# A block with two transformer layers, one core: the first feed-forward layer's down projection partly by seven products

## The reference, cut to what matters

```python
SEQ = 512
D_MODEL = 1024
D_FF = ((8 * D_MODEL // 3 + 255) // 256) * 256      # 2816
...
def first_block(x, positions, ...):
        ...
        x = x + rms_norm(y, post_mix_norm[l])
        h = rms_norm(x, pre_ffn_norm[l])
        f = (jax.nn.silu(h @ w_gate[l]) * (h @ w_up[l])) @ w_down[l]
        x = x + rms_norm(f, post_ffn_norm[l])
    return x
```

## Time and profile before

| | |
|---|---|
| median of 3 runs | 1816.99 us (1814.9 to 1817.48) |
| the profiled execution | 1819.24 us, of which its span is 1817.44 |
| TensorE, matmuls | busy 98% of the span, granted clock 0.998 of full |
| VectorE, ScalarE, GpSimd | busy 61%, 46%, 19% |
| transfers | 230.85 MB, mean 127 GB/s |

### The profile page before, as it was taken

One profiled execution on the slowest core, in us unless ns is written; L12 is line 12 of the kernel. 1 busy time (PEld: TensorE's weight loads), 2 busy tenths in 40 slices (PEclk: granted clock), 3 DMA queues, 4 the chain that ended last, 5 costly groups with the idle time before them and its releaser, 6 DMA issues.

```text
span 1817.4 us, 24673 instructions
## 1 busy us (share of the span) xinstructions
PE 1783.8 (98%) x9586; PEld 1452.3 (80%) x9586; DVE 1113.3 (61%) x1763; ACT 834.6 (46%) x1593; POOL 336.7 (19%) x404
## 2 busy tenths in 40 slices
PE   7999999999999999999999999999999999999998
PEld 7767898888888877878878786667788998888886
DVE  6655643233345787887778745677556357574747
ACT  5346533222224555554555544554435445342435
POOL 1503000000000046254462640000020012112120
PEclk9999999999999999999999999999999999999999
DMA  7211333323332454352443444233543248849482
GB/s 246 80 59 62 97 114 116 93 93 93 93 93 75 151 142 131 120 152 95 154 140 117 143 158 152 82 102 119 139 149 123 76 145 191 229 107 257 114 208 70
DMA packets 140419, 230.85 MB, mean 127 GB/s; under 512 B 27264, under 2 KB 59456, under 8 KB 139664
## 3 DMA queue, kind: packets, MB, share of 16 engines
q1 hardware_dynamic: 118944, 166.70, 29.2%
q0 software_dynamic: 20496, 60.10, 12.5%
q10 hardware_dynamic: 864, 2.49, 0.3%
HBM read 216.54 MB, written 12.71 MB: 126 GB/s over the span
## 4 chain that ended last, share of the span: by engine, by line
PE 78%; DVE 12%; DMA 3%; ACT 3%; issue 2%; POOL 1%; SPq 0%; DVEq 0%; ACTq 0%; POOLq 0%
PE m L2134 13%; PE m L2136 13%; PE m L2135 13%; PE m L2145 6%; PE m L2147 6%; PE m L2146 6%; PE s L2297 3%; DVE lo L1395 3%; DMA raw<-in_w_up_dram 3%; PE m L2269 2%; PE m L2242 2%; PE m L2244 2%; PE m L2243 2%; PE m L2271 1%; PE m L2270 1%
## 5 line engine op out<-in xcount | busy, mean ns | idle before, releaser
L2134 PE MATMUL m<-hH,hi 128*128 128x512 f32 (+1 forms) x1392 | 530.6, 381 | 3.2 <-DVE hL L1425 1.6
L2136 PE MATMUL m<-hH,lo 128*128 128x512 f32 (+1 forms) x1392 | 509.8, 366 | 0.0
L2135 PE MATMUL m<-hL,hi 128*128 128x512 f32 (+1 forms) x1392 | 509.1, 366 | 0.0
L1395 DVE TENSOR_TENSOR lo<-raw,hi 128x1024 fp32r<-128x1024 f32 x267 | 335.9, 1269 | 193.0 <-ACT hi L915 192.6
L915 ACT ACTIVATE hi<-raw 128x1024 fp32r<-128x1024 f32 x267 | 276.1, 1050 | 205.3 <-DMA raw<-in_w_up_dram 64.9
L2134 PEld LDWEIGHTS m<-hH,hi 128*128 128x128 f32 x1392 | 263.3, 189 | 51.2 <-issue 4.5
L2136 PEld LDWEIGHTS m<-hH,lo 128*128 128x128 f32 x1392 | 263.1, 189 | 43.4
L2135 PEld LDWEIGHTS m<-hL,hi 128*128 128x128 f32 x1392 | 263.7, 189 | 38.9
L2145 PE MATMUL m<-hi,hH 128*128 128x512 f32 (+1 forms) x320 | 133.8, 418 | 1.6 <-DVE lo L1395 1.6
L2147 PE MATMUL m<-hi,hL 128*128 128x512 f32 (+1 forms) x320 | 122.4, 383 | 0.0
L2146 PE MATMUL m<-lo,hH 128*128 128x512 f32 (+1 forms) x320 | 122.4, 382 | 0.0
(11 more groups left out here) (330 smaller groups left out, 3032.9 us busy)
## 6 DMA issues: line engine op xcount, KB each, us to landing
raw<-in_w_in_dram SPq DMA_DIRECT2D x72, 512.0 KB, 3.7
wq<-in_w_down_dram POOLq DMA_DIRECT2D x40, 512.0 KB, 10.0
hn<-scr_cs_dram POOLq DMA_DIRECT2D x32, 512.0 KB, 4.3
raw<-in_w_up_dram SPq DMA_DIRECT2D x32, 512.0 KB, 5.9
wq<-in_w_down_dram SPq DMA_DIRECT2D x24, 512.0 KB, 7.6
raw<-in_w_gate_dram SPq DMA_DIRECT2D x44, 256.0 KB, 2.8
raw<-in_w_up_dram SPq DMA_DIRECT2D x44, 256.0 KB, 3.1
raw<-in_w_down_dram SPq DMA_DIRECT2D x22, 512.0 KB, 4.0
```

The source lines that it names most:

```text
L1395: e.tensor_tensor(d, r, h.bitcast(F32), ALU.subtract).then_inc(s_lo, 1)
L2134: e.matmul(bank, wh[:, kk, c], h[:, k, q], start=k == 0, stop=False)
L2135: e.matmul(bank, wh[:, kk, c], l[:, k, q], start=False, stop=False)
L2136: x = e.matmul(bank, wl[:, kk, c], h[:, k, q], start=False, stop=k == kt - 1)
```

## The change

The rows 0 to 1791 of `w_down` (gu blocks 0 to 6) are now multiplied by two blocks of the seven-product kind: `ds0` for 768 rows (quarters of 384, that is three tiles of 128, so that the second unit of a quarter is half a unit) and `ds1` for 1024 rows. The last 1024 rows keep their blocks `dn20` and `dn21`. The code of the fs blocks is made general over `SEVEN = ds0, ds1, fs0 .. fs3`.

- `dn00`, `dn01` (24 slots) and `dn10`, `dn11` (32 slots) go; `ds0` (28 slots, of six and three matmuls in turn) and `ds1` (28 slots of six) come.
- The products of gate and up of the blocks gu0 to gu6 are no longer split at once; they go whole into new buffers `fa1`, and their parts are split into slices of `aH` and `aL`.
- Quarters of `w_down` need eight more buffers: `WQ0` takes the two `hn`, the four token rows of `X`, `gain0` and a new `wqf`. So `X` is stored to HBM when `gu0` begins (`scr["x"]`) and loaded again in `gu7`.
- SyncE loads the first quarters among the weights of `gu1` and `gu2`, behind a wait for that store and for the transposes of the normed `X`; those for `ds1` among the weights of `gu3` and `gu4`. The loads of two gains, which stood among the weights of `gu2`, move behind to those of `gu8` (`gains()`).

```diff
-FF1 = [(0, 3), (3, 4), (7, 4)]
+FF1 = 7
+SEVEN = ["ds0", "ds1"] + [f"fs{f}" for f in range(NFF2)]
...
-    for c, (b0, nb) in enumerate(FF1):
-        for b in range(b0, b0 + nb):
-            add(f"gu{b}", "fm" if b else "half", 4, "dddd")
-        for h in range(2):
-            add(f"dn{c}{h}", "tmt" if c == 2 and h else "tm", nb, "dddd" if c else "aaaa")
+    for b in range(11):
+        add(f"gu{b}", "fm" if b else "half", 4, "dddd")
+        if b in (2, 6):
+            add(f"ds{b // 4}", "fs", 14, "d" * 14)
+    for h in range(2):
+        add(f"dn2{h}", "tmt" if h else "tm", 4, "dddd")
...
+SEVEN_K = [3, 4] + [4] * NFF2
+SEVEN_ROW = [0, 768] + [1024 * f for f in range(NFF2)]
+WQ_AFTER = [("gu1", 2), ("gu3", 3), ("up0", 8)] + [(f"up{2 * f}", 3) for f in range(1, NFF2)]
+WQ_BEFORE = {BLK[name].u0 + u + i: (f, i) for f, (name, u) in enumerate(WQ_AFTER) for i in range(4)}
...
+        FA1 = [sb(f"fa1{j}", [128, 4, S], c=P2) for j in range(2)]
+        WQ0 = [x[:, :].rearrange("p (k n) -> p k n", k=2) for x in HN] + [X[:, t, :].rearrange("p (k n) -> p k n", k=2) for t in range(4)]
+        WQ0 += [G[0][:, :].rearrange("p (k n) -> p k n", k=2), sb("wqf", [128, 2, 512], c=P2)[:, :, :]]
...
             def load_quarter(f, i):
                 w, j, n = (("d", 1, 1), ("b", 0, 1), ("a", 0, 0), ("c", 1, 0))[i]
...
                 for x in range(2):
                     if f == 0:
+                        o.wait_ge(s_ntr, 16)
+                        o.wait_ge(s_hn, 16)
+                        o.wait_ge(s_xsv, 16)
+                        o.wait_ge(s_mlo, 8)
+                    elif f == 2:
                         o.wait_ge(s_ntr, 44)
...
-                if n[:2] == "gu" and i >= 2:
+                if n[:2] == "gu" and int(n[2:]) >= FF1 and i >= 2:
...
+                    d = s[:, :]
+                    if i >= 2 and g < FF1:
+                        c = g // 3
+                        if c:
+                            o.wait_ge(s_flo, rests(1))
+                        c = min(c, 1)
+                        k = 2 * (g - 3 * c) + i - 2
+                        d = FA1[k // SEVEN_K[c]][:, k % SEVEN_K[c], :]
+                    e.tensor_tensor(d, s[:, :], bank[:, :], ALU.mult).then_inc(s_evd, 1)
...
+                    first = (f, t, h) not in added
...
+                    if first and not f:
+                        e.tensor_scalar(x, bank[:, :], -1.0 if i // 2 in FS_MINUS else 1.0, None, ALU.mult).then_inc(s_evd, 1)
...
+                if g == s0("gu0") + 2:
+                    o.wait_ge(s_xup, 8)
+                    e.dma_start(scr["x"], X[:, :, :].rearrange("p t d -> p (t d)")).then_inc(s_xsv, 16)
+                if g == s0("gu7") + 2:
+                    o.wait_ge(s_lo, BLK["ds1"].u0 + 12)
+                    e.dma_start(X[:, :, :].rearrange("p t d -> p (t d)"), scr["x"]).then_inc(s_xbk, 16)
```

More of the change, by code:

```diff
@@ L197, in conversions @@
         s = -1 if j < 4 else max(free[j - NHL] + 1 + more if j >= NHL else 8, at[-1] + 1, first[j] - (8 if BLK["xq"].u0 <= j < BLK["xo"].u0 else 14))
-        for f in range(NFF2):
-            b = BLK[f"fs{f}"]
+        for name in SEVEN:
+            b = BLK[name]
             s = max(s, b.s0 + FS_CONV[j - b.u0]) if j - b.u0 in FS_CONV else s
@@ L512, in build @@
         s_gs, s_ahi, s_alo, s_rl = (sem(f"s_{n}") for n in ("gs", "ahi", "alo", "rl"))
-        s_fhi, s_flo, HID = s_ahi, s_alo, 2 * sum(nb for _, nb in FF1)
+        s_fhi, s_flo = s_ahi, s_alo
         s_cwt, s_cw, s_cid, s_tanh, s_silu = (sem(f"s_{n}") for n in ("cwt", "cw", "cid", "tanh", "silu"))
@@ L665, in build, with fa, sums, part @@
         fL = [sb(f"fL{i}", [128, 4, 256], F32R, c=P8) for i in range(4)]
-        WQ = [x[:, :].rearrange("p (k n) -> p k n", k=2) for x in HN] + [sb(f"wq{i}", [128, 2, 512], c=P8)[:, :, :] for i in range(6)]
+        WQ2 = [x[:, :].rearrange("p (k n) -> p k n", k=2) for x in HN] + [sb(f"wq{i}", [128, 2, 512], c=P8)[:, :, :] for i in range(6)]
         P8.close()
         FS2 = G[1][:, :].rearrange("p (k t) -> p k t", k=4)
-        def fa(i, j):
-            return FA[j - 1][:, :, 256 * i - 256:256 * i]
+        def fa(f, i, j):
+            return (FA if f >= 2 else FA1)[j - 1][:, 0:SEVEN_K[f], 256 * i - 256:256 * i]
+        def sums(f):
+            return FS2[:, 0:SEVEN_K[f], :]
+        def part(f, p):
+            return [fa(f, 1, 1), fa(f, 1, 2), sums(f), fa(f, 1, 1), fa(f, 2, 1), fa(f, 1, 2), fa(f, 2, 2)][p]
+        def split_part(n):
+            if n < 14:
+                return tuple(x[:, 2 * (n % 4):2 * (n % 4) + 2, :].rearrange("p a (b c) -> p (a b) c", b=2) for x in (aH, aL))
+            return fH[n % 4], fL[n % 4]
+        def wq(f, w, x):
+            return (WQ2 if f >= 2 else WQ0)[WQ_I[w] + x][:, 0:unit_tiles(f, x), :]
+        def quarter(f, j, c, x):
+            w = A["w_down_2"][0] if f >= 2 else A["w_down"][0]
+            r0 = SEVEN_ROW[f] + 128 * (SEVEN_K[f] * j + 2 * x)
+            return w[r0:r0 + 128 * unit_tiles(f, x), 512 * c:512 * c + 512].rearrange("(k p) n -> p k n", p=128)
         def landed(f, w, n):
@@ L680, in landed @@
                 return s_wq[WQ_I[w] // 2], WQ_FROM + 32 * f + 32
-            return s_wd[WQ_I[w] // 2], WD_FROM + 32 * ((WQ_PER[w] - 1) * f + n - 1)
+            return s_wd[WQ_I[w] // 2], (WD_FROM if f >= 2 else 0) + 32 * ((WQ_PER[w] - 1) * f + n - 1)
         def rows(w, u, c0, c1):
@@ L1410, in norm_scale @@
                     o.wait_ge(s_ntr, 2 * n - 2)
+                if 8 <= n < 12:
+                    o.wait_ge(s_lo, BLK["ds1"].u0 + 8)
                 if n >= 12:
@@ L2239, in block @@
                         claim("main", i % 4)
-                    for kk in range(2):
+                    for kk in range(unit_tiles(n // 7, x)):
                         k = 2 * x + kk
-                        e.matmul(m[:, :], fH[n % 4][:, k, q], wh[:, kk, :], start=k == 0 and p in FS_FRESH, stop=False, skip_group_check=True)
-                        e.matmul(m[:, :], fH[n % 4][:, k, q], wl[:, kk, :], start=False, stop=False, skip_group_check=True)
-                        y = e.matmul(m[:, :], fL[n % 4][:, k, q], wh[:, kk, :], start=False, stop=k == 3, skip_group_check=True)
+                        e.matmul(m[:, :], hh[:, k, q], wh[:, kk, :], start=k == 0 and p in FS_FRESH, stop=False, skip_group_check=True)
+                        e.matmul(m[:, :], hh[:, k, q], wl[:, kk, :], start=False, stop=False, skip_group_check=True)
+                        y = e.matmul(m[:, :], hl[:, k, q], wh[:, kk, :], start=False, stop=k == last, skip_group_check=True)
                     finish(y, b, i if x else None, j if t == 1 else None)
```

174 lines of the change are left out of this document (91 added, 83 removed).

## The result

The changed kernel takes **1820.86 us** (median of 8 runs, 1817.47 to 1824.72), the kernel before 1816.8 in the same comparison (8 runs, 1814.9 to 1817.48): ratio 1.0023, 95% interval [1.0014, 1.0032]. It is slower by 4 us, where 1812.4, that is 4.4 us less than before, was forecast. The profiled execution took 1820.16 us, 0.92 more than that of before (1819.24, which lies above all eight timed runs of that kernel).

The account below looks back on a forecast made before the run. TensorE was taken as the bound, matmul count times 0.2266 us. Saving -9.5, stalls +4.0 and +0.9 give -4.6: the profiled 1819.24 becomes 1814.6, on the median's scale 1812.4 us, range 1807.3 to 1817.3.

Parts of the forecast that it names:

- What bounds the kernel: Where the change works, TensorE bounds: time is the number of matmuls times their pace, 0.2266 us from start to start.
- The saving: In the down projection, 42 fewer matmuls at 0.2266 us each save 9.5 us if TensorE keeps its pace.
- What is hidden: VectorE's work in ds0 keeps ahead of TensorE, by 1 us at the tightest point, and costs nothing.
- The first stall, at the start of gu1: Unit 35 lands at 249.1, so gu1's first matmul waits for its bank: 4.0 us, bounds 0 and 10.7.
- The burst behind fs0: Loads from 1555.30, whose second unit landed 13.0 us after the start; taken as the measure for unit 35's landing.
- The second stall, at the start of gu4: Unit 60 lands 20.2 us after ds0's end, ahead of gu3's sigmoids, so gu4 waits 0.9 us.
- the sum: Saving and two stalls: -9.5 + 4.0 + 0.9 = -4.6 us.
- My bound of 3.9: Upper bound in us of the stall at gu4's start, if the burst takes 3 us more.
- The gain is eaten: GpSimd's additions slow unit 35: stall 6 to 7 us at gu1, 2 to 3 at gu4; 1816.5 to 1817.5; chance 0.22.
- Slower: Unit 35, behind SyncE's wait, lands after 258.2, 22 us after the burst starts; time 1821 us; chance 0.06.
- The bursts are hidden: Unit 35 lands by 245.1 and unit 60 by 19 us after ds0; full 9.5 us kept, 1807.5; chance 0.22.

Follow-up runs that it names:

- unit 35 later: The changed kernel with ScalarE's split of unit 35 one slot later, behind gu0's last sigmoid: 1816.54 us, ratio 0.9997 to the kernel before.
- quarters later: The changed kernel with SyncE loading ds0's quarters from gu2 on and ds1's from gu4's third unit on: 1809.61 us, ratio 0.9958.
- unit 57 later: The changed kernel with unit 57's split and rest one slot later, behind the copy of ds0's last bank to Y: 1821.64 us, ratio 1.0023.
- the run without them: The changed kernel with units 35 and 57 each one slot later and GpSimd's additions for ds1 cut to 8 of 128 partitions: 1809.09 us, ratio 0.9952.
- the runs with copies added: The kernel before with six, three or one ScalarE copies ahead of gu0's first sigmoid: 1825.72, 1823.32 and 1818.15 us.
- the first three runs: The changed kernel with unit 35's split one slot later, with unit 57's, and with both: 1816.54, 1821.64 and 1816.14 us.
- additions cut: The changed kernel in its own order, GpSimd's additions of quarters for ds0 and ds1 cut to 8 of 128 partitions: 1818.26 us, ratio 1.0006.
- both later: The changed kernel with the splits of units 35 and 57 each one slot later: 1816.14 us, ratio 0.9995.

## Why the prediction was wrong, step by step

**What bounds the kernel** and **The saving** held. With the pauses out of the way the 42 matmuls gave 9.52 us, predicted 9.5.

**What is hidden** held: ds0 has no gap. In its window TensorE is busy throughout, VectorE for 27.49 of 28.5 us, so it is nearly the bound there:

```profile
298.40:326.90 28.50, 28.50 (x127) 23.59 (x126) 27.49 (x36) 14.77 (x19) 1.39 (x2) 1.00 0.36 84
```

**The first stall, at the start of gu1** held in place, chain and size: unit 35 in ScalarE's hands at 248.82 (predicted 249.1), pause 3.67 (4.0). The burst behind fs0 was the right ruler for it, and moving either end of the chain (unit 35 later, quarters later) takes it away.

**The second stall, at the start of gu4** is the step that failed, in place and in size. Its unit landed where I had put it: ScalarE has unit 60 at 347.03, 20.0 us after ds0's end (20.2 predicted). But another wait stood ahead of it. I followed ScalarE from ds0's end to gu3's sigmoids and did not do the same for VectorE, where the rest of unit 57 stands ahead of the last copy to `Y`. That gave 2.6 us where 0.9 were in the sum, and by making gu4 later it hid the stall that I had foreseen: gu3's sigmoids now wait for TensorE until 349.26, 1.2 us behind unit 60's split. The runs with unit 57 later show this from the other side: take the one away and the other comes up, with 5.1 us, as unit 60 then lands 24 us after ds0's end; GpSimd's additions are issued there at 325.39 and 339.95 for 327.00 and 341.95, and the run without them has no pause. My bound of 3.9 for it was too low as well.

**What the sum left out** is the clock. Each of the two pauses is followed by 3.41 us at half clock, 1.7 and 1.8 us. That is 3.5 us in all, and the sum had no term for it. With the pauses as measured and the clock, the forecast's sum would have been -9.5 + 3.7 + 2.6 + 3.5 = +0.3; the two profiled executions show +0.9, with a fall near 660 us that lasted twice as long.

The medians are 4.1 us apart. Most of the 3.1 us between the two figures is that the profiled execution of before took longer than is usual for that kernel: 1819.24 is 2.4 us above that kernel's median, and 1820.16 is 0.7 below the changed kernel's. How such an execution can come about is shown by the runs with copies added, which differ from the kernel before in nothing up to 245 us: two of them are at full clock 1.5 us earlier, and one has no fall near 660, worth another 1.6. What stays open is why the timed runs of the changed kernel gather higher, up to 1824.7: its three profiles lie at 1817.45, 1820.16 and 1821.77, and none of them shows such an execution. The timed runs of the four kernels with a pause made by transfers at gu1, in gu3 or at gu4 (the changed one and the first three runs) spread over 7 to 8.5 us in 8 to 11 runs each, those without any over 2.3 to 3.5 in 5 or 6; but a kernel with pauses from SyncE's order alone (additions cut) spreads over 3.5 too, in 11, and the kernel before, with no pause, over 2.6 to 6.6 in its four sets of 8 to 27. That was seen and not explained.

**The rivals.** "The gain is eaten" (1816.5 to 1817.5) was nearer than the forecast, for the wrong reason: at gu1 the additions account for 0.7 to 1.2 us of the pause and unit 35 was not later than forecast. Where they do decide, at gu4, is in the runs with unit 57 later. "Slower" named 1821, nearly the time measured, but that is luck: it was tied to one mechanism (unit 35 after 258.2), which did not occur. Two middling stalls and their clock used up the saving, and the rest is the part left open above. "The bursts are hidden" comes about if the quarters are loaded two and three units later: 1809.6, or 1808.5 with unit 57 moved as well; it was put at 1807.5.

## What to carry to other kernels

Price a stall of TensorE with what follows it: in this kernel every step of 3.3 us and more brought a fall of the clock, worth 1.7 us for most of them, most steps of 2.5 to 2.9 did too, and steps of 1.9 in steady work did not. Where a burst of loads stands ahead of weights that are wanted soon, walk through every in-order engine that touches them, the one that writes the rest as well as the one that splits, and look which bank or table stands behind. And read the DMA share over the whole stretch, not one landing: when it is near 1, later weights will be late too, and moving one wait helps only where none of them holds a bank (unit 35 here, but not unit 57, where only moving or removing bytes helped).

## What the runs showed of the hardware

The granted clock of a TensorE that was busy at full clock fell to 0.50, for 3.41 or 6.83 us, at all nine steps of 3.27 us and more in the fourteen profiles (3.27, 3.40, 3.48, 3.56, 3.79, 4.15, 5.33, 5.98 and 7.41 us): behind the step or near its end, and in the two steps of 5.33 and 7.41 us already 1.2 and 2.7 us before it. Of the fifteen steps of 2.5 to 2.9 us twelve had a fall, from 0.3 us before their end to 1.5 behind it, and three had none (2.53, 2.68 and 2.70). Ten of these fifteen are the step near 655 us that every profile of the changed kernel and its variants has (2.72 in the rows above), so the fall near 660 has a pause ahead of it as the others do. In the kernel before and the three runs with copies the steps there are of 2.0 and 2.35 us, and the fall came in three of the four. It did not come behind steps of 1.00 (gu3), 1.48 (gu4) and 1.97 (gu1), nor behind the one of 1.88 us near 77 us that every profile has; but in the run with three copies one of 2.06 us, begun at 11.6, has a fall from 14.8 us behind it. So at about 2 to 2.7 us it goes either way; near 660 TensorE also works in short pieces (3.19 us busy in the 6.8 ahead of the fall in the kernel before), and no run tells what part that has:

```profile
655.30:662.10 6.80, 3.19 (x26) 2.24 (x26) 6.70 (x5) 5.11 (x13) 5.68 (x7) 1.00 0.72 182
```

In the three runs with a step over 5 us (unit 57 later, both later, six copies) there was no fall near 660; I have no explanation for that. Full pace at the start came for good between 11.7 and 19.8 us in the fourteen profiles, up to 2.8 us of the time. The Trainium skill ("TensorE: Matmul & The Clock Gate", Part 1) says that this start differs from run to run of the same kernel; the profiles agree: the three of the changed kernel have it at 11.7, 17.4 and 18.1 us. The transfers of this core moved 386 GB/s in a window of 3.4 us (253.0 to 256.4) and 265 in one of 32 us, both of the changed kernel.
